# Memory keys and values of both layers projected between the units of the even attention

## The reference

```
for layer in range(2):
    h = h + 0.5 * swiglu(rmsnorm(h, g), wg, wu, wd)
    h = h + mixer(rmsnorm(h, mix_g))                     # even in layer 0, odd in layer 1
    h = h + memory_xattn(rmsnorm(h, mg), rmsnorm(mem, sg), wq, wkv, qg, kg, wo)
    h = h + 0.5 * swiglu(rmsnorm(h, g2), wg2, wu2, wd2)
```

## Time and profile before

| | |
|---|---|
| median of three runs | 1821.94 us |
| the three runs | 1797.82, 1821.94, 4195.58 us |
| profiled execution, its time | 1794.75 us |
| its span | 1792.9 us |
| mean granted clock of TensorE | 0.952 |
| TensorE busy | 1680.8 us, 94% of the span |
| VectorE, ScalarE busy | 1069.4 us, 848.0 us |

### The profile page before, as it was taken

The page is one execution under the profiler, slowest core; times in us unless marked ns, Lnnn a source line. Parts: engine busy times, 40 slices in busy tenths (PEclk is TensorE's granted clock), DMA queues, the critical chain, the costliest instruction groups (busy, mean ns, idle before and its releaser), DMA issues.

```text
span 1792.9 us, 25005 instructions
## 1 busy us (share of the span) xinstructions
PE 1680.8 (94%) x10388; PEld 1508.4 (84%) x10388; DVE 1069.4 (60%) x1551; ACT 848.0 (47%) x1215; POOL 12.8 (1%) x19
## 2 busy tenths in 40 slices
PE   7969898899998999997979999999999999999998
PEld 7867787799978998785767899879998877789996
DVE  4547566588846554576747655546554775755553
ACT  4446543566535443453336544444443554654441
POOL 0000000000000000000000000000000000000000
PEclk9969999899998999997589999999999999999999
DMA  7723255455553555452034445545555432425553
GB/s 269 274 102 124 78 204 188 142 177 187 188 189 140 188 179 196 166 185 97 1 115 144 159 176 184 188 171 181 188 188 188 165 141 95 159 100 179 177 188 115
DMA packets 42928, 290.21 MB, mean 162 GB/s; under 512 B 5000, under 2 KB 5150, under 8 KB 9920
## 3 DMA queue, kind: packets, MB, share of 16 engines
q1 hardware_dynamic: 38272, 271.93, 42.8%
q0 software_dynamic: 4544, 16.69, 2.8%
HBM read 287.51 MB, written 8.55 MB: 165 GB/s over the span
## 4 chain that ended last, share of the span: by engine, by line
PE 90%; DVE 5%; ACT 2%; DVEq 2%; DMA 1%; issue 1%; SPq 0%; POOL 0%; POOLq 0%; ACTq 0%; PEldq 0%
PE bank L443 26%; PE bank L444 25%; PE bank L445 25%; PE bank L449 8%; PE bank L705 2%; PE bank L1295 2%; DVEq L1990 2%; DVE low L411 1%; DMA raw<-stream_dram 1%; PE bank L595 1%; ACT high L400 0%; PE bank L456 0%; DVE u L924 0%; DVE h L1000 0%; DVE u L648 0%
## 5 line engine op out<-in xcount | busy, mean ns | idle before, releaser
L400 ACT ACTIVATE high<-raw 128x2048 fp32r<-128x2048 f32 x257 | 489.0, 1914 | 560.9 <-DMA raw<-stream_dram 557.8
L411 DVE TENSOR_TENSOR low<-raw,high 128x2048 fp32r<-128x2048 f32 x255 | 581.5, 2289 | 268.5 <-ACT high L400 267.4
L443 PE MATMUL bank<-xh,high 128*128 128x256 f32 x1880 | 535.5, 285 | 1.1 <-DVE low L411 1.1
L444 PE MATMUL bank<-xl,high 128*128 128x256 f32 x1880 | 534.1, 284 | 0.0
L445 PE MATMUL bank<-xh,low 128*128 128x256 f32 x1880 | 534.1, 284 | 0.0
L443 PEld LDWEIGHTS bank<-xh,high 128*128 128x128 f32 x1880 | 363.4, 193 | 2.1 <-issue 2.1
L444 PEld LDWEIGHTS bank<-xl,high 128*128 128x128 f32 x1880 | 363.3, 193 | 0.0
L445 PEld LDWEIGHTS bank<-xh,low 128*128 128x128 f32 x1880 | 363.1, 193 | 0.0
L443 PE MATMUL bank<-high,xh 128*128 128x512 f32 (+2 forms) x528 | 205.0, 388 | 2.2 <-DVE low L411 1.1
L444 PE MATMUL bank<-low,xh 128*128 128x512 f32 (+2 forms) x528 | 203.0, 385 | 0.0
L445 PE MATMUL bank<-high,xl 128*128 128x512 f32 (+2 forms) x528 | 202.8, 384 | 0.0
(11 more groups left out here) (207 smaller groups left out, 1578.5 us busy)
## 6 DMA issues: line engine op xcount, KB each, us to landing
raw<-stream_dram SPq DMA_DIRECT2D x257, 1024.0 KB, 4.8
band_wide_dram<-band_rows_dram POOLq DMA_DIRECT2D x1, 3072.0 KB, 23.0
t_wide_dram<-t_rows_dram POOLq DMA_DIRECT2D x1, 2304.0 KB, 15.3
u<-mem_dram POOLq DMA_DIRECT2D x2, 1024.0 KB, 5.3
bias<-band_wide_dram POOLq DMA_DIRECT2D x1, 2048.0 KB, 9.6
rel_wide_dram<-rel_rows_dram POOLq DMA_DIRECT2D x1, 1920.0 KB, 16.7
bias<-t_wide_dram POOLq DMA_DIRECT2D x1, 1536.0 KB, 7.8
bias<-rel_wide_dram POOLq DMA_DIRECT2D x1, 1280.0 KB, 7.0
```

The source lines that it names most:

```text
L400: act.activation(self.high[:, n % RING, :], self.raw[:, n % RING, :], ACT.Copy).then_inc(self.high_split, 1)
L411: dve.tensor_tensor(self.low[:, n % RING, :], self.raw[:, n % RING, :], self.high[:, n % RING, :].bitcast(F32), ALU.subtract).then_inc(sel ...
L443: pe.matmul(out, lh, rh, start=start, stop=False)
L444: pe.matmul(out, lh, rl, start=False, stop=False)
```

## The change

The stage that projected keys and values is gone from both layers. In its place:

- The memory rows are loaded twice, early: into `o` beside the MLA projection, where `Rope` takes the squares, and at its end the inverse root, of their norms; and into `u` beside `Lambda`.
- In `Select`, TensorE turns the rows (16 transposes, from the fifth unit on), ScalarE rounds them, VectorE subtracts: once for both layers.
- The eight slots of `wkv0` and `wkv1` stand in the stream before `even_out`. The gain per layer is multiplied into these weights when they are split, in four pieces per slot (`gained`).
- After each of the 16 units of the even attention TensorE does one part (`MemoryFill`): 4 tiles, 12 matmuls of 512 columns, into bank 7. Two parts complete a group (layer, keys or values, block of 128 rows), which ScalarE drains with the row factor into `u` (layer 0) or `gain` (layer 1). A slot is released by the second block's part.
- `memory_stages` has one projection less: `wq`, with the norms of the keys at its start (`early`) and those of the queries at its end.

```diff
-            plan += [("even_tail", KT, S), ("even", 7 * KT, HALF), ("even_out", 2 * KT, HALF)]
+            plan += [("even_tail", KT, S), ("even", 7 * KT, HALF), ("wkv0", 2 * KT, HALF), ("wkv1", 2 * KT, HALF),
+                     ("even_out", 2 * KT, HALF)]
         else:
             plan += [("odd", 6 * KT, HALF), ("odd_out", 2 * KT, HALF)]
-        plan += [(f"wq{layer}", KT, HALF), (f"wkv{layer}", 2 * KT, HALF), (f"wo{layer}", 8, HALF)]
+        plan += [(f"wq{layer}", KT, HALF), (f"wo{layer}", 8, HALF)]
...
+        self.gained = {}
+        for layer in range(2):
+            m, n = self.plan[f"wkv{layer}"], ROWS.index(f"l{layer}_src") * KT
+            for i in range(0, m.count, m.per):
+                self.gained[m.slot(i)] = n + i % KT
...
+            if n in self.gained:
+                for cut, gain in self.gained_pieces(n):
+                    last = act.activation(self.high[:, n % RING, cut], self.raw[:, n % RING, cut], ACT.Copy, scale=gain)
+                last.then_inc(self.high_split, 1)
+            else:
+                act.activation(self.high[:, n % RING, :], self.raw[:, n % RING, :], ACT.Copy).then_inc(self.high_split, 1)
             self.act_next = n + 1
+    def gained_pieces(self, n):
+        for j in range(SLOT // HALF):
+            k = self.gained[n] + j
+            yield slice(j * HALF, (j + 1) * HALF), PARAM(self.param, "gains")[:, k:k + 1]
...
+            if n in self.gained:
+                for cut, gain in self.gained_pieces(n):
+                    last = dve.scalar_tensor_tensor(self.low[:, n % RING, cut], self.raw[:, n % RING, cut], gain,
+                                                    self.high[:, n % RING, cut].bitcast(F32), ALU.mult, ALU.subtract)
...
+        self.turn = Turn(core, ([early] if early else []) + (batches or [None] * len(jobs)), base=4)
...
+            if n == 0 and self.early:
+                self.turn.turn_rows(pe, s, 0)
...
+        if self.early:
+            self.turn.square_rows(act, s, 0)
...
+        if self.early:
+            c.split_low(dve, self.jobs[0][0].slot(0) - LEAD)
+            self.turn.scale_rows(dve, s, 0, step)
...
+def start_memory(c, pool, dst, dram):
+    pool.dma_start(dst, dram["mem"].rearrange("(b p) d -> p b d", p=P)).then_inc(c.mem_loaded, 16)
+class MemoryProject(Project):
+    def __init__(self, core, x, jobs, memory, dram):
+        super().__init__(core, x, jobs)
+        self.memory, self.dram = memory, dram
+    def gpsimd(self, pool, s):
+        start_memory(self.core, pool, self.memory, self.dram)
...
+def memory_rows(c):
+    return c.u[:, :, 0:D]
+def memory_kv(c, layer):
+    return c.gain if layer else c.u[:, :, D:2 * D]
+class MemoryRows:
+    BANKS = (4, 5, 6, 7)
+    def __init__(self, core):
+        self.core = core
+    def tile(self, k):
+        return self.core.bank[self.BANKS[k // 2]][:, (k % 2) * S:(k % 2 + 1) * S]
+    def tensor(self, pe, s, pair):
+        c = self.core
+        if pair == 0:
+            pe.wait_ge(c.mem_loaded, 32)
+        for k in (2 * pair, 2 * pair + 1):
+            for b in range(NB):
+                last = pe.transpose(self.tile(k)[:, block_cut(b)], memory_rows(c)[:, b, k * P:(k + 1) * P], c.ident)
+        last.then_inc(s["mem_turned"], 1)
+    def scalar(self, act, s, pair):
+        c = self.core
+        act.wait_ge(s["mem_turned"], pair + 1)
+        ps = c.bank[self.BANKS[pair]][:, :].rearrange("p (k q) -> p k q", k=2)
+        act.activation(c.xh[:, 2 * pair:2 * pair + 2, :], ps, ACT.Copy).then_inc(s["mem_high"], 1)
+    def vector(self, dve, s, pair):
+        c = self.core
+        dve.wait_ge(s["mem_high"], pair + 1)
+        ps = c.bank[self.BANKS[pair]][:, :].rearrange("p (k q) -> p k q", k=2)
+        cut = slice(2 * pair, 2 * pair + 2)
+        dve.tensor_tensor(c.xl[:, cut, :], ps, c.xh[:, cut, :].bitcast(F32), ALU.subtract).then_inc(s["mem_low"], 1)
+class MemoryFill:
+    BANK = 7
+    def __init__(self, core, units):
+        self.core = core
+        groups = [(layer, n, b) for layer in range(2) for n in range(2) for b in range(NB)]
+        assert units == 2 * len(groups)
+        self.parts = [(g, *group, range(half * KT // 2, (half + 1) * KT // 2))
+                      for g, group in enumerate(groups) for half in range(2)]
+    def tensor(self, pe, s, i):
+        c = self.core
+        group, layer, n, b, ks = self.parts[i]
+        m = c.plan[f"wkv{layer}"]
+        if group and ks.start == 0:
+            pe.wait_ge(s["mem_stored"], group)
+        for k in ks:
+            w = c.piece(pe, m, n * KT + k)
+            last = mm3(pe, c.bank[self.BANK][:, :], (c.xh[:, k, block_cut(b)], c.xl[:, k, block_cut(b)]), w,
+                       k == 0, k == KT - 1)
+            if b == NB - 1:
+                c.release(last, m, n * KT + k)
+            elif k == KT - 1:
+                last.then_inc(s["mem_filled"], 1)
+    def scalar(self, act, s, i):
+        c = self.core
+        group, layer, n, b, ks = self.parts[i]
+        m = c.plan[f"wkv{layer}"]
+        c.split_high(act, m.slot(n * KT + ks.stop - 1))
+        if ks.stop < KT:
+            return
+        if b == NB - 1:
+            act.wait_ge(c.slot_used, m.slot(n * KT + KT - 1) + 1)
+        else:
+            act.wait_ge(s["mem_filled"], 2 * layer + n + 1)
+        act.activation(memory_kv(c, layer)[:, b, n * HALF:(n + 1) * HALF], c.bank[self.BANK][:, :], ACT.Copy,
+                       scale=c.inv[:, 6 + b:7 + b]).then_inc(s["mem_stored"], 1)
+    def vector(self, dve, s, i):
+        group, layer, n, b, ks = self.parts[i]
+        m = self.core.plan[f"wkv{layer}"]
+        self.core.split_low(dve, m.slot(n * KT + ks.stop - 1))
...
+            if self.filler and i < len(units):
+                self.filler.tensor(pe, s, i)
...
+        dve.wait_ge(s["norm_squares"], NB)
+        dve.tensor_scalar(c.inv[:, 6:8], c.inv[:, 6:8], 1.0 / D, EPS, ALU.mult, ALU.add).then_inc(s["norm_means"], 1)
+        dve.wait_ge(s["norm_roots"], 1)
+        dve.reciprocal(c.inv[:, 6:8], c.inv[:, 6:8])
+    def scalar(self, act, s):
+        c = self.core
+        act.wait_ge(c.mem_loaded, 16)
+        for b in range(NB):
+            act.activation(c.o[:, b, :], c.o[:, b, :], ACT.Square, accum_out=c.inv[:, 6 + b:7 + b])\
+               .then_inc(s["norm_squares"], 1)
+        self.copy_high(act, s, 0)
+        act.wait_ge(s["norm_means"], 1)
+        act.activation(c.inv[:, 6:8], c.inv[:, 6:8], ACT.Sqrt).then_inc(s["norm_roots"], 1)
...
+            if i >= 4:
+                self.memory.tensor(pe, s, i - 4)
...
+                self.memory.vector(dve, s, i - 4)
...
+    def __init__(self, core, dram):
+        super().__init__(core)
+        self.dram = dram
+    def gpsimd(self, pool, s):
+        start_memory(self.core, pool, memory_rows(self.core), self.dram)
...
-    wkv, wq, wo = c.plan[f"wkv{layer}"], c.plan[f"wq{layer}"], c.plan[f"wo{layer}"]
-    mem = c.u[:, :, 2048:3072]
+    wq, kv = c.plan[f"wq{layer}"], memory_kv(c, layer)
     x = (c.xh, c.xl)
-    keys, queries = head_batch(c, 0, HALF, 0, f"mk{layer}", P), head_batch(c, D, HALF, 4, f"mq{layer}", P)
-    both = (keys[0] + queries[0], keys[1] + [(g[0] + NB, *g[1:]) for g in queries[1]])
-    out = [Project(c, x, [(wq, 0, range(KT), HALF, [u[:, b, D:D + HALF] for b in range(NB)])],
-                   source=Source(c, c.h, x, gain=f"l{layer}_mem", norm=True), scale=True),
-           Project(c, x, [(wkv, n * KT, range(KT), HALF, [u[:, b, n * HALF:(n + 1) * HALF] for b in range(NB)])
-                          for n in range(2)], source=Source(c, mem, x, gain=f"l{layer}_src", norm=True), scale=True,
-                   batches=[both, None])]
+    keys = head_batch(c, 0, HALF, 0, f"mk{layer}", P, kv)
+    queries = head_batch(c, 2 * D, HALF, 4, f"mq{layer}", P)
+    out = [Project(c, x, [(wq, 0, range(KT), HALF, [u[:, b, 2 * D:2 * D + HALF] for b in range(NB)])],
+                   source=Source(c, c.h, x, gain=f"l{layer}_mem", norm=True), scale=True, batches=[queries], early=keys)]
...
-    st.append(Attention(c, units, select))
+    st.append(Attention(c, units, select, filler=MemoryFill(c, len(units))))
```

More of the change, by code:

```diff
@@ L906, in scalar @@
                            scale=c.inv[:, 2:3] if self.scale else 1.0).then_inc(s["drained_by_act"], 1)
-            if self.turn.batches[n][0]:
+            if self.turn.batches[n + self.early][0]:
                 self.rows_there(act, s, n)
-                self.turn.square_rows(act, s, n)
+                self.turn.square_rows(act, s, n + self.early)
+            if n == 0 and self.early:
+                self.turn.copy_high(act, s, 0)
             if n:
-                self.turn.copy_high(act, s, n - 1)
-        self.turn.copy_high(act, s, len(self.jobs) - 1)
+                self.turn.copy_high(act, s, n - 1 + self.early)
+        self.turn.copy_high(act, s, len(self.jobs) - 1 + self.early)
     def vector(self, dve, s):
@@ L927, in vector @@
             i.then_inc(s["drained_by_dve"], 1)
```

(33 more changed lines are left out.)

28 lines of the change are left out of this document (15 added, 13 removed).

## The result

Twenty runs of each kernel: 1818.68 us median after (1813.22 to 1826.39, and one of 8498) against 1819.05 before (1791.43 to 1827.64, and one of 4196). The ratio was 1.010, 95% interval 1.007 to 1.014. The ratio leaves out runs over 1.5% above a kernel's fastest, which are many of before's; the medians of all runs are equal. So by the interval the changed kernel is 1% slower, where I had it 0.2% faster, and 1818.7 lies just above my range. The profiled execution took 1814.18 us (span 1812.4).

A forecast was written before the change was run, and what follows sets the result against it. TensorE, busy 94% of the span, was taken as the bound, at half clock in the even attention. Memory stages -30.2, even attention +22.5, selection +3.1 and Rope +0.9 gave -3.7 us: 1791 us from 1794.75, range 1775 to 1818.

The forecast's parts named there:

- my sum: Whole kernel: -30.2 + 22.5 + 3.1 + 0.9 = -3.7 us on the profiled 1794.75 us, giving 1791 us.
- GpSimd's issue at 0.7 us: Two memory loads issued by GpSimd, 0.7 us each, beside stages of 2 us and more; no cost added.
- the memory stages: Both layers: removing the memory projection gains 36.2 us, less 6 us for the clock, so -30.2 us.
- The query stage: Both layers: key norms first, layer 0's query drain 2.1 us later, then 7.9 us from drain to memory attention.
- The half-clock rival: Memory attentions stay at half clock: +9.2 instead of +3 us in each layer, giving 1803 us; chance 0.20.
- The even attention: Filler lifts its clock; 80.4 us against 59.4 plus 1.5 us of waits: +22.5 us.
- held-up-units rival: Even attention: ScalarE's and VectorE's splits hold up the units, +6.5 us more, giving 1797 us; chance 0.14.
- doesn't bound on average: Even attention: VectorE has 59 us of work in a stage of 80 us, so it isn't the limit on average.
- Selection: Selection stage: four added VectorE subtractions, 2.8 us, and a first wait of 0.3 us: +3.1 us, from 2 to 5.
- Rope: Rope stage: mean, root and reciprocal of the memory rows after the last copy, +0.9 us, up to 3.
- The rule on transposes: The clock rises right behind 16 transposes, against the Trainium skill's rule that transpose mode doesn't engage the full clock.
- The slower rival: Even attention: the filler doesn't lift the clock, 192 matmuls cost 0.456 us each, +64 us, giving 1855 us; chance 0.05.

The follow-up runs named there:

- a_load_keep: Changed kernel with two extra matmuls per unit in the first attention, and the second memory load moved from the lambda stage to the even projections: 1788.8 us.
- b_keep_fill: Kernel before with two extra matmuls per first-attention unit, plus 24 ahead of the even attention's units and one in each; no projection moved: 1789.0 us.
- a_same: The changed kernel as it is, run again beside others: 1 of 12 runs kept the first attention's clock, at 1793.2 us.
- a_keep: Changed kernel with two extra matmuls of 256 columns after each turn in the first attention's 28 units: 1796.9 us.

## Why the prediction was wrong, point by point

- **The stretch that decided it was not in my sum.** I wrote that in the first attention the clock is 0.50 before the dense matmuls "and 0.99 after them, for 48 us with none added", and took what one execution showed for what the kernel does. It does so in 53 of 153 runs; in the other 100 the clock is taken to fall there, as it does in every profiled run of a long time, and the run is 25 us longer. I also read the shown runs, 1821.94 against a lowest of 1797.82, as a scatter with the profiled one "at the foot". It was two groups, 25 us apart, and the larger one was the upper. So the step that failed is the base of the sum: from the median of all runs, 1819.05, the same -3.7 gives 1815.4, and the range would have reached higher with it. Compared within groups (1.2 and 1.7 us), or with the clock held (3.7 us), the change is slightly faster; a measured ratio above 1 comes from the 6 of 19 runs of before that kept the clock where the changed kernel had none. Why it had none is open (5 of 49 above).
- **The sum itself, -3.7, came out as -3.45 in the trace and -3.7 in the runs with the clock held; three of its terms were off and cancelled, which is luck.** Missed: +5.4 in the lambda stage. I had costed GpSimd's issue at 0.7 us "beside stages of 2 us and more" and not asked when its queue would let the stage end. a_load_keep gave that back. Missed too: +1.35 in even_out, which I had at nothing, since the trace before had the clock back there. Too small by 4.6: the memory stages, -34.8 for -30.2 (-17.0 and -17.8 for -15.4 and -14.8). The -17.8 holds all that follows, and 1.0 of it is no work of the change: layer 1's turns ahead of its query projection took 3.3 us before and 2.3 after.
- **The query stage** went as described, key turns first. Before the drain VectorE held it up for 1.7 us in layer 0 (8.7 us from the inverse to the drain, for 7.1) and 2.3 in layer 1 (8.7 for 6.4), where I had 2.1 and 2.7. From its drain at 1009.58 to the first score it was 7.4 us for my 7.9. The clock fell in the stop and came back with the end of the scores (0.50 in 1014 to 1022, 0.94 in 1022 to 1026). The half-clock rival (never recovering) is out; +2.2 measured for my +3.
- **The even attention**: 22.1 for my 22.5, and the parts hold too. From start to start, the 192 filler matmuls take 47.5 us (my 43.8, and 2.7 for the first part at half clock) and the units' own work 30 (my 29.6). TensorE has no hole but 0.7 us in 905 to 925, so the held-up-units rival (+6.5) didn't come, and that VectorE "doesn't bound on average" held. It held because the filler is there: b_keep_fill, without it, waits 3.8 us for VectorE.
- **Selection** +2.5 for +3.1; **Rope** nothing measurable for +0.9.
- **The rule on transposes.** I read from one row that the clock rises right behind 16 transposes. It does so in even_out in 15 of the 18 profiled runs and not in the other three (the changed kernel, its repetition a_same, and a_keep), though the transposes take 3.68 us in all three, as in the kernel before. There the clock comes back six to seven matmuls of 512 columns later. The Trainium skill ("TensorE: Matmul & The Clock Gate", Part 4 (PE-mode transpose)) says that the full clock doesn't engage in transpose mode. By that rule the trace of the changed kernel agrees (half clock until 971.18) and that of the kernel before doesn't (1.00 from 914.5 on), so neither my reading nor the rule holds throughout.
- The slower rival that I named (a filler that doesn't lift the clock, 1855) was the right kind of mechanism in the wrong place: half clock in an attention of small matmuls, but in the one 700 us earlier.

## What to carry to other kernels

Before a profile is used as the base of a sum, put its time beside all runs shown: two groups with a gap mean that some stretch goes one of two ways, and the profile shows only one. Then look in it for long stretches of small matmuls at full clock and hold the clock there (two dense matmuls for a unit here, some 7 us for 25 at stake; one wasn't enough) before anything of 4 us is compared. Work that is moved under a stage "to lift its clock" should be held against plain filler matmuls: here 40 of them did as much as 192 useful ones moved. A load issued by GpSimd belongs in a long stage.

## What the runs showed of the hardware

- The granted clock fell from 1.00 to 0.50 between 144 and 156 us with TensorE busy without a gap, and stayed low for some 50 us of the same small matmuls (six profiled runs), or it didn't fall at all (the others). The times of one and the same kernel, the one before, fall into two groups to match, 100 and 53 of 153. One added matmul of 256 columns in each unit: low in 12 of 12 runs; two: full in 72 of 72. What tips it isn't settled: the load, the semaphores and later code showed no effect in 12 runs each (4, 6 and 4 kept), the norms in the Rope stage are suspected (5 of 49), and no run changed them alone. It wasn't tried to shift the stage's start by small steps.
- A stage in which GpSimd only issues a load of 1 MB ended 6.8 us after the issue, by the chain of waits (851.11 to 857.86), though nobody in that stage wanted the rows. The load landed after 6.6 us; with it in a longer stage the wait is gone.
- In the changed kernel's trace the clock came back in the memory attention after 12 score instructions of 256 columns, all at half clock, and in the even attention during the first 9 filler matmuls of 512 columns (0.63 us each at half clock, 0.39 from 886.17 on).
- The same pauses and instructions don't always leave the same clock. Behind a pause of some 5 us and 16 transposes, ahead of even_out, it was full in 15 profiled runs and half in three. Behind a pause of 2.70 us of TensorE ahead of layer 0's query projection the 16 turns took 2.33 us in the kernel before (clock 1.00) and 3.06 us in the changed one (0.62 in 994.5 to 997.2).
